# Expert rows stored without their norm, the norm applied to each gathered set, and the second expert's rows turned inside the first one's third product

## The reference, cut to what matters

```python
h2 = rms(x, p['g_ffn']) * (1 + sc2) + sh2      # rms: x / sqrt(mean(x^2) + eps) * g
aff = softmax(h2 @ w_router)                   # per token, over 16 experts
gate, idx = top_k(aff.T, cap)                  # cap: 64 latent + 16 context tokens per expert
xg = h2[idx]                                   # 80 gathered rows of 2048
y = (silu(xg @ w_e1) * (xg @ w_e3)) @ w_e2 * gate
x = x + gate2 * scatter_add(y, idx)
```

## Time and profile before

| | us |
|---|---|
| median of three runs | 3423.59 |
| the profiled execution | 3426.3 |
| its span | 3424.5 |
| PE busy | 3277.5 (96%) |
| DVE busy | 2097.1 (61%) |
| ACT busy | 1401.0 (41%) |
| POOL busy | 367.1 (11%) |
| projections end, experts begin | about 2249.1 |
| first product of an expert begins | 2303.8 |
| the loop's first body begins | 2359.3 |

### The profile page before, as it was taken

The page is one execution under the profiler, slowest core; times in us unless marked ns, Lnnn a source line. Parts: engine busy times, 40 slices in busy tenths (PEclk is TensorE's granted clock), DMA queues, the critical chain, the costliest instruction groups (busy, mean ns, idle before and its releaser), DMA issues. The chain is left out here.

```text
span 3424.5 us, 39938 instructions
## 1 busy us (share of the span) xinstructions
PE 3277.5 (96%) x16068; PEld 2541.8 (74%) x16068; DVE 2097.1 (61%) x1827; ACT 1401.0 (41%) x1293; POOL 367.1 (11%) x437
## 2 busy tenths in 40 slices
PE   6989999999999999989999999949999999999997
PEld 4778888888887999987888888725666666666664
DVE  3346555565551777753233243257888888888987
ACT  3221222221211444432121222236777777777775
POOL 0020010020001000000011111030111111211112
PEclk9999999999999999999999999969999999999999
DMA  9565554485553010125353444358999999999999
GB/s 378 210 184 193 204 180 173 162 265 189 194 187 111 33 43 34 41 83 213 114 175 135 152 168 147 108 210 320 376 396 377 387 397 397 383 384 398 395 394 338
DMA packets 143614, 790.13 MB, mean 231 GB/s; under 512 B 19120, under 2 KB 30416, under 8 KB 62816
## 3 DMA queue, kind: packets, MB, share of 16 engines
q1 hardware_dynamic: 101680, 668.72, 50.7%
q0 software_dynamic: 41808, 119.60, 11.6%
HBM read 720.39 MB, written 67.86 MB: 230 GB/s over the span
## 5 line engine op out<-in xcount | busy, mean ns | idle before, releaser
L102 DVE TENSOR_TENSOR w_lo<-w_stage,w_hi 128x2048 fp32r<-128x2048 f32 x379 | 865.4, 2288 | 138.3 <-ACT w_hi L97 138.3
L97 ACT ACTIVATE w_hi<-w_stage 128x2048 fp32r<-128x2048 f32 x379 | 727.4, 1920 | 305.6 <-PE e_ps L109 305.6
L107 PE MATMUL i_ps<-w_hi,hT_hi 128*128 128x512 f32 (+1 forms) x1440 | 564.9, 392 | 6.2 <-ACT evacuated L479 3.8
L109 PE MATMUL i_ps<-w_hi,hT_lo 128*128 128x512 f32 (+1 forms) x1440 | 556.0, 386 | 0.0
L108 PE MATMUL i_ps<-w_lo,hT_hi 128*128 128x512 f32 (+1 forms) x1440 | 555.8, 386 | 0.0
L107 PE MATMUL e_ps<-w_hi,xgT_hi 128*80 128x512 f32 x1024 | 404.3, 395 | 2.5 <-DVE xgT_lo L2101 2.3
L108 PE MATMUL e_ps<-w_lo,xgT_hi 128*80 128x512 f32 x1024 | 403.9, 394 | 0.0
L109 PE MATMUL e_ps<-w_hi,xgT_lo 128*80 128x512 f32 x1024 | 401.5, 392 | 0.0
L107 PE MATMUL p_ps<-w_hi,xT_hi 128*128 128x512 f32 x960 | 378.5, 394 | 6.9 <-DVE xT_lo L1577 6.9
L109 PE MATMUL p_ps<-w_hi,xT_lo 128*128 128x512 f32 x960 | 374.7, 390 | 0.0
L108 PE MATMUL p_ps<-w_lo,xT_hi 128*128 128x512 f32 x960 | 374.4, 390 | 0.0
(11 more groups left out here) (329 smaller groups left out, 4424.4 us busy)
## 6 DMA issues: line engine op xcount, KB each, us to landing
w_stage<-in_w_e SPq DMA_DIRECT2D x384, 1024.0 KB, 9.1
w_stage<-in_w_ada SPq DMA_DIRECT2D x96, 1024.0 KB, 6.6
w_raw<-in_w_in SPq DMA_DIRECT2D x64, 1024.0 KB, 5.0
w_stage<-in_w_o_gm SPq DMA_DIRECT2D x16, 1024.0 KB, 6.9
w_stage<-in_w_o_mla SPq DMA_DIRECT2D x16, 1024.0 KB, 5.1
w_stage<-in_w_out SPq DMA_DIRECT2D x16, 1024.0 KB, 4.9
acts<-evacuated POOLq DMA_DIRECT2D x60, 256.0 KB, 4.8
side<-acts POOLq DMA_DIRECT2D x40, 256.0 KB, 5.5
```

Of the source, the lines that this page charges most:

```text
L97: act.activation(dst, src, ACT.Copy).then_inc(st.hi, 1)
L102: dve.tensor_tensor(dst, src, hi.bitcast(F32), ALU.subtract).then_inc(st.split, 1)
L107: pe.matmul(out, x_hi, w_hi, start=first, stop=False)
L109: return pe.matmul(out, x_lo, w_hi, start=False, stop=last)
```

## The change

- In the projections each block of xg is stored to h2 in DRAM by POOL as soon as it is made (20 stores of 256 KB), without inv and without the shift. h2 gets 16 more columns.
- In the last block, `turn_xg` and `route` of the early tiles stand between the dense products of the later tiles.
- ACT warms the table of Sqrt in the projections and the table of Exp right behind Sqrt in the router. `scale_rows` and POOL's shift additions and stores of whole rows are gone.
- DVE copies inv 16 times beside each other and SP stores it to the 16 new columns of h2, so a gathered row brings its own inv as column 2048.
- New `rows_scaled(e, g)` on DVE: xg * inv + shift in place, for column groups of 768, 768 and 512 on 80 partitions. In a body it comes at pieces 9, 10 and 11 for expert i+2, and its first group waits for the gather. PE's `turn_rows` waits for it and no longer for the gather.
- The gathers of experts 0 and 1 read `rows` directly, without the copy. DVE splits weight pieces 0 and 1 ahead of the first `rows_scaled`, and piece 2 behind it. PE starts the first product when the first group is split.
- Expert 1's rows are turned behind pieces 10 and 13 of expert 0, into their own tiles (`xT2_hi`, `xT2_lo`), and body(0) uses these.

```diff
@@ phase_projects, POOL
+                if s == OUT:
+                    for t in range(TT):
+                        pool.wait_ge(xg_ok, TT * i + t + 1)
+                        pool.dma_start(M.h2[bass.ts(t, P), bass.ts(i, NC)].rearrange("p (j n) -> p j n", j=KG), M.xg[i][t]).then_inc(M.h2_stored[i], 16)
@@ phase_projects, ACT
+            act.activation(ones[:, 0:1], M.ident[:, 0:1], ACT.Sqrt)
@@ phase_projects, PE
+                    if n == N_PIECES - 1:
+                        if t >= 1:
+                            turn_xg(N_CH - 1, t - 1)
+                        if t >= 2:
+                            route(N_CH - 1, t - 2)
-            for t in range(TT):
-                turn_xg(N_CH - 1, t)
-                if t:
-                    route(N_CH - 1, t - 1)
+            turn_xg(N_CH - 1, TT - 1)
+            route(N_CH - 1, TT - 2)
             route(N_CH - 1, TT - 1)
@@ phase_experts, SP
-            for r in range(2):
-                sp.dma_start(shift[:, r, :], M.mod[r:r + 1, 3 * D:4 * D].to_broadcast((P, D))).then_inc(shift_in, 16)
+            sp.wait_ge(inv, 2)
+            sp.dma_start(M.h2.rearrange("(t p) n -> p t n", p=P)[:, :, D:D + 16], inv_rows[:]).then_inc(inv_out, 16)
...
@@ phase_experts, POOL
+            def gather_first(e):
+                pool_wait(pool, x_tr, 3 * e + 3, passed)
+                pool.indirect_dma_start(out=xg[:], out_offset=None, in_=M.h2,
+                                        in_offset=bass.IndirectOffsetOnAxis(ap=rows[:, e:e + 1], axis=0)).then_inc(gathered, 16)
-            pool.wait_ge(shift_in, 32)
...
             for t in range(TT):
-                pool.wait_ge(scaled, 4 * t + 4)
-                pool.tensor_tensor(h_row[t % 3][:], h_row[t % 3][:], shift[:, min(t, 1), :], ALU.add).then_inc(h_ok, 1)
-                pool.wait_ge(h_ok, t + 1)
-                pool.dma_start(M.h2[bass.ts(t, P), :], h_row[t % 3][:]).then_inc(h_out[t % 3], 16)
...
             pool.wait_ge(pick_ok, 2)
-            gather(0)
-            gather(1)
+            gather_first(0)
+            gather_first(1)
@@ phase_experts, ACT
-            act.wait_ge(inv, 1)
-            scale_rows(0)
+            act.activation(sm[:, 2, 0:1], M.ident[:, 0:1], ACT.Exp).then_inc(warm, 1)
+            act.wait_ge(warm, 1)
@@ phase_experts, DVE
+            def rows_scaled(e, g):
+                if g == 0:
+                    dve.wait_ge(gathered, 16 * e + 16)
+                c = slice(TXG[g][0] * P, TXG[g][1] * P)
+                dve.scalar_tensor_tensor(xg[:, c], xg[:, c], xg[:, D:D + 1], shift[:, c], ALU.mult, ALU.add).then_inc(x_sc, 1)
@@ body(i) on DVE
                     if j == 8:
                         hidden_lo(i)
+                    if j in (9, 10, 11) and rows:
+                        rows_scaled(i + 2, j - 9)
@@ ahead of the loop, DVE
-            for j in range(LEAD):
-                lo(j, j, None)
+            lo(0, 0, None)
+            lo(1, 1, None)
+            dve.wait_ge(shift_in, 32)
+            for g in range(3):
+                rows_scaled(0, g)
             for g in range(3):
                 rows_lo(0, g)
+            lo(2, 2, None)
             for j in range(N0):
                 lo(j + LEAD, j + LEAD, None)
+                if j in (4, 5, 6):
+                    rows_scaled(1, j - 4)
...
@@ turn_rows on PE
-                if g == 0:
-                    pe.wait_ge(gathered, 16 * e + 16)
...
+                pe.wait_ge(x_sc, 3 * e + g + 1)
@@ ahead of the loop, PE
             for q in range(PB):
                 up(PB + q, q, (PB + q) % NW, pair[1])
-            for g in range(3):
-                turn_rows(1, g)
-            with pe.Fori(0, EXPERTS - 2) as i:
+                if q == 2:
+                    turn_rows(1, 0)
+                    turn_rows(1, 1)
+                if q == 5:
+                    turn_rows(1, 2)
+            body(0, (xT2_hi, xT2_lo))
+            with pe.Fori(1, EXPERTS - 2) as i:
                 body(i)
```

More of the change, by code:

```diff
@@ L1350, in phase_projects @@
     M.xg.append([wide(third_xg[:, t, :] if t < 4 else more[:, t, :]) for t in range(TT)])
-    M.xg.append([by_j(last_xg, t) for t in range(TT)])
+    M.xg.append([wide(last_xg[:, t, :]) for t in range(TT)])
     N_CH = D // NC
@@ L1374, in phase_projects @@
         shift_mul, shift_sum, shift_ok = sem("shift_mul"), sem("shift_sum"), sem("shift_ok")
+        M.xn_stored, M.h2_stored = stored, [M.pool_sem(f"proj_h2_stored{i}") for i in range(D // NC)]
         clear_finished(nc, M)
@@ L1794, in phase_experts @@
     m = Map(nc, M.phase_at)
[L1795 to L1799, removed]
+    xg = m.new("xg", [SLOTS, D + 16], F32)
     xT_hi, xT_lo = (m.new(f"xgT_{h}", [P, KT, SLOTS], F32R) for h in ("hi", "lo"))
+    second = Map(nc, M.phase_at + X_END)
+    xT2_hi, xT2_lo = (second.new(f"xgT2_{h}", [P, KT, SLOTS], F32R) for h in ("hi", "lo"))
+    shift = Map(nc, M.x_raw_at + 4 * D).new("shift2_rows", [SLOTS, D], F32)
     sil = m.new("silu_a", [SLOTS, D_FF], F32)
@@ L1877, in last @@
                         load(n + 4 * c + q, (j0 + 4 * c + q) % NS, E2[e, c, q])
-            for r in range(2):
-                sp.dma_start(shift[:, r, :], M.mod[r:r + 1, 3 * D:4 * D].to_broadcast((P, D))).then_inc(shift_in, 16)
+            sp.wait_ge(inv, 2)
+            sp.dma_start(M.h2.rearrange("(t p) n -> p t n", p=P)[:, :, D:D + 16], inv_rows[:]).then_inc(inv_out, 16)
+            for i in range(2):
+                sp.wait_ge(M.h2_stored[i], 16 * TT)
+            for a, b, r in ((0, CAP_LAT, 1), (CAP_LAT, SLOTS, 0)):
+                sp.dma_start(shift[a:b, :], M.mod[r:r + 1, 3 * D:4 * D].to_broadcast((b - a, D))).then_inc(shift_in, 16)
             for q in range(4, PB):
+                if q == PB - 1:
+                    for t in range(TT):
+                        sp.wait_ge(M.xn_stored[t], 16 * 2 * (D // NC))
                 load(q, q, E13[0][0, q])
-            sp.wait_ge(scaled, 4 * TT)
             for a, b, r in ((0, CAP_LAT, 1), (CAP_LAT, SLOTS, 0)):
@@ L2025, in _ @@
                                accum_out=sm[:, 2, t:t + 1]).then_inc(ex, 1)
-            for t in range(1, TT):
-                scale_rows(t)
-            act.wait_ge(scaled, 4 * TT)
             for j in range(LEAD):
+                if j == 2:
+                    act.wait_ge(M.h2_stored[2], 16 * TT)
                 hi(j, j, None)
@@ L2284, in turn_rows @@
             def turn_rows(e, g):
-                if g == 0:
-                    pe.wait_ge(gathered, 16 * e + 16)
-                    if not (isinstance(e, int) and e == 0):
-                        pe.wait_ge(sil_ok, e)
-                if g == 2:
+                pe.wait_ge(x_sc, 3 * e + g + 1)
+                first = isinstance(e, int) and e == 0
+                if g == 0 and not first:
+                    pe.wait_ge(sil_ok, e)
+                if g == 2 and not first:
                     pe.wait_ge(x_lo, 3 * e + 1)
@@ L2350, in down_plain, with body @@
                 ins.then_inc(s.used, 1)
-            def body(i, rows=True):
+            def body(i, turned=(xT_hi, xT_lo), rows=True):
                 n0 = NP * i + N0
@@ L2383, in _ @@
                 turn_rows(0, g)
-            pe.wait_ge(x_lo, 3)
             for q in range(PB):
+                for g in range(3):
+                    if TXG[g][0] == 2 * q:
+                        pe.wait_ge(x_lo, g + 1)
                 up(q, q, q % NW, pair[0])
```

70 lines of the change are left out of this document (39 added, 31 removed).

## The result

The changed kernel takes 3437.06 us, the median of five runs (3431.84 to 3447.18), beside 3423.64 for the kernel before on the same chip: ratio 1.0039, 95% interval 1.0029 to 1.005. It is 0.39% slower. The prediction said 3419.4 and most likely faster; the time lies inside its range, on the side of rival C.

What follows compares the result with a forecast made beforehand. PE (busy 96%) was taken as the bound, with gains outside the full loop: 3426.3 - 13.4 - 9.65 + 18.9 = 3422.15 us profiled, 2.7 lower as median, so 3419.4; range 3404 to 3440.

Steps and rivals of the forecast that it cites:

- rival C: Loop: POOL's late gather holds DVE in most bodies; slower from six late bodies, eight 3431.8, thirteen 3447 us; chance 0.23.
- playing through of low halves 13 to 15: Loop body: with the scaling between them these low halves still end before PE wants them, with 0.2 us to spare.
- Part 1: Router: Exp table 3.1, last softmax scaling 4.2, index cast 1.1 us sooner, less 0.45; picks ready 7.95 us earlier.
- Part 3: Second expert's row turning: 7.25 us of stop saved plus 2.4 for the low clock behind it, 9.65 together.
- Part 4: Loop: DVE's scaling waits for the gather, low half 13 queues behind it and PE stops; price 18.9 us.
- The gain as a whole: Before the loop: 13.4 us from an earlier first product and 9.65 from the second expert's rows, 23.05 together.
- four late bodies: Loop bodies 1 to 13: four gathers land late, where eight of thirteen POOL copies were late in the old trace.
- The price of a late body: Loop: PE stops 3.1 + 0.5 = 3.6 us; 2.4 more for a lowered clock was left as a possibility.
- The price of an early body: Loop: PE stops 0.1 us for low half 13 and another 0.4 for 14 and 15, 0.5 together.
- A: The forecast itself: a mix in the loop, 3 to 6 late bodies, 3416 to 3426 us; chance 0.38.
- The first gather: Behind the router: issue held by two low halves, landing 5.5 us after issue, first product at 2290.4, 13.4 us sooner.
- rival D: Behind the router: first gather not held by DVE, issued at 2277.8 instead of 2281.4, 3415.8 us; chance 0.10.
- The projections' end: Ahead of the router: last tile's turning waits on three DVE instructions, 0.45 us later, bounds 0 and 1.5.

## Why the prediction was wrong

**Right.** The place of both gain and loss, and the mechanism of the loss: DVE stands at the first scaling, low half 13 is late, PE stops for it. The scaling's own time costs next to nothing, as the prediction's playing through of low halves 13 to 15 had it: 0.1 us per body in the kernel with the gather ahead, where it had 0.2 to spare. Part 1: the two stretched instructions and the table load gave 8.33 us between the start of the phase and the low halves where 8.4 were predicted. Part 3: 9.65 predicted, 10.0 measured by undoing it. The play: where PE stops for low half 13, its stop is DVE's wait less 0.53 us (1.78 gives 1.25, 0.98 gives 0.45, 3.83 gives 3.30), as Part 4 had worked out; the 0.53 come back in small steps at the low halves behind it. The gain as a whole, 21.8 us against 23.05, is near in part by luck: the first product came 2.9 us later than predicted, and the shorter low clock behind it, which no part had counted, gave back about 1.5.

**The step that failed** is in Part 4: "I take four late bodies: 13 x 0.5 + 4 x 3.1 = 18.9 us". It was 39.0. Three of its terms were too small.
- The count. In the profiled execution six were late. Four was taken instead of the old eight because the relieved DMA engines would land the scatters sooner. They landed 14.3 us behind their issue in the median (12.6 to 14.7) where it was 14.5 (11.1 to 15.2); whether these 0.2 us made six out of eight, or chance did, stays open. The count also changes from run to run, as the 15 us between the fastest and the slowest of the five runs suggest; that was not traced. The median run is 5.1 us below the profiled one, which would be about one late body less (an estimate: 5.36 less 0.97 is 4.4 for each). By the prediction's own prices six late bodies cost 25.1.
- The price of a late body. It was set at 3.6, and the low clock was left to rival C as something possible. DVE waited 3.56 us on average and the body was 5.36 longer: 0.19 there anyway, and 1.6 for the clock. Each of the six stops brought the low level. The row that the prediction used for this had a stop of 3.83 us; the stops here were 2.6 to 3.3. It is not a fixed price: in the kernel with only the wait at piece 9 a stop of 2.50 us cost nothing beyond itself.
- The price of an early body, 0.5: it was 0.97, since the gathers landed about as late as assumed but with waits of 0.77 on average, and 0.19 came on top, the play being used up by the wait.

None of the three alone makes the kernel clearly slower. By the count alone the sum gives 3425.6; with the clock, 9.7, it is 3435.3, and with the early bodies' 3.3 it is 3438.6. That this is near the measured 3437.1 is partly luck, since these terms come from an execution that took 3442.18. Its own account closes: 3426.3 - 2.68 - 21.8 + 39.0 + 0.7 is 3441.5, and 0.6 more lie outside the span. Rival C had the place, the point (six) and the clock in it, and got 0.23 where A got 0.38. The only ground for fewer than the old eight was the relief of the DMA engines, and no row of before could measure it.

**The first gather.** The prediction had it held by the two low halves, and it was: issued until 0.87 us behind their end. The landing took 7.5 us behind the issue's end where 5.5 was taken, outside the bounds of 4.5 and 6.9; with the projections' end 0.75 worse than counted that makes the first product 2.9 us later than predicted, after the 2.68 are taken off. That the hold is DVE's doing, and not the price of an issue at that place, is shown by the pair of kernels above: 4.25 us with DVE's low halves from the start, 2.97 where they began with the issue, 0.98 where they came behind it. The Trainium skill, page SBUF — State Buffer, section Who interferes with whom, says that a tensor_tensor with both inputs in SBUF blocks only GpSimd's reads, and infers that descriptor generation goes on beside it. The inference does not carry over to the issue of an indirect DMA, and rival D, which carried it over, fails. Two ordinary DMAs that POOL issued beside a low half took their usual 0.54 us each in the changed kernel:

```profile
2114.36 2.29 DVE L1581 TENSOR_TENSOR w_lo<-w_stage,w_hi 128x2048 fp32r<-128x2048 f32 x1 [0.59 <-ACT w_hi L1504]
```

```profile
2114.59 1.07 POOL L1452 DMA_DIRECT2D gate<-mod  x2
```

An indirect DMA differs in that it reads its row numbers from SBUF, and reads are what the page says is blocked. This fits, but no run separates that reading from the rest of the issue.

**The projections' end.** 0.45 later was counted, 1.2 came, inside the bounds; undoing the edit gave the 1.2 back in the trace (0.9 in the span) and nothing that the medians can tell.

## What to carry to other kernels

When work is hung onto the arrival of a transfer in the strict order of an engine, ask first what stands behind it on that engine, and put it where the transfer has landed in its slowest case, not in its usual one: three pieces later the same instructions cost 0.19 us per body, and the change was worth 0.5% instead of -0.4%. When a stop's price is worked out for a TensorE that is otherwise always busy, count the low clock behind it too, as a range (here stops of 1.85 and of 2.62 us had it, stops of 1.25 and of 2.50 had not), and take the count of late cases from the old trace unless a row measures the relief. An experiment that moves one wait can make another: read in its profile who waited before its time is used for or against a theory.

## What the runs showed that was not expected

- PE's stops of 2.6 to 3.3 us in the changed kernel were each followed by the low level (0.50 to 0.68 in the 2 us right behind them), and so was one of 1.85 us in another. A stop of 1.25 us was not, and neither was one of 2.50 (1.00 behind it). So the length of the stop alone does not decide it.
- A semaphore that POOL raises behind an indirect DMA came before the issue had begun (DVE went on at 2276.34, the issue began at 2276.52); a small copy behind it came when the issue was over (2277.55, issue from 2276.57 for 0.98).
- A low half that had already begun and its direct follower held the issue for both (until 0.87 us behind the second). Where the first began just ahead of the issue, the issue got in between the two (until 0.9 us behind the first).
- A low half that is late by 0.1 to 0.2 us makes each body of all these kernels longer than before, and PE's busy time does not show it: only the distance between the starts of its products does (0.37 and 0.30 where 0.23 is usual).
- Not settled: what decides whether a scatter lands in time for an early body, and what beyond the length of a stop decides on the clock behind it.
